# Up projections of the two convolution FFNs: 512-column matmuls from the third pair on, over an input that already holds the norm's factor

## Chip, cores and metric

The kernel runs on one core of one Trainium2 chip. The metric is the time of one execution on the device in microseconds (us). Engines are named as in the profile: PE is TensorE (matmuls), PEld its weight loads, DVE is VectorE, ACT is ScalarE, POOL is GpSimd, SP is SyncE, which issues the DMAs of the weights.

## What is computed

One sequence of 256 tokens with 1024 channels goes through seven phases: attention and pooling (L0), FFN F0, sliding-window attention (L1), FFN F1, then FFN F2, a mixer with convolution and attention (MIX), and FFN F3. All is in float32. The change touches F0 and F1, which the reference computes so:

```python
def rms_norm(x, g):
    xf = x.astype(jnp.float32)
    y = xf * lax.rsqrt(jnp.mean(xf * xf, axis=-1, keepdims=True) + EPS)
    return (y * g.astype(jnp.float32)).astype(x.dtype)

def conv_glu_ffn(x, norm_g, w_up, conv_w, conv_b, w_down):
    S = x.shape[1]
    h = rms_norm(x, norm_g) @ w_up
    hp = jnp.pad(h, ((0, 0), (CONV_W - 1, 0), (0, 0)))
    c = conv_b
    for j in range(CONV_W):
        c = c + conv_w[j] * hp[:, j:j + S]
    gate, up = jnp.split(c, 2, axis=-1)
    return x + (jax.nn.silu(gate) * up) @ w_down
```

`CONV_W` is 3, `w_up` is 1024 x 5632 and `w_down` 2816 x 1024. F2 and F3 have the same shapes, but no convolution.

## The kernel before

**Precision.** Every float32 product is made of three matmuls in the type fp32r: an operand is split into a high part (a copy in fp32r) and a low part (the operand less its high part), and high x high, high x low and low x high are summed in PSUM. Channels lie on the 128 partitions, tokens along the free axis, so an activation tile has 256 columns.

**Weights.** They come in 172 chunks, most of 128 x 2048 (1 MB). SP loads chunk i into one of 3 buffers `raw`, once the low part of chunk i-3 is made (`s_lo`). ACT makes the high part `whi` (`high(i)`, once PE is done with chunk i-4, `s_used`), DVE the low part `wlo` (`low(i)`). PE waits for `wlo` of a chunk before its first matmul with it.

**An FFN.** Chunks c0 to c0+21 are the up projection, two for each of 11 pairs p (two gate tiles in one, two up tiles in the other, by position e); chunks c0+22 to c0+32 are the down projection. In `half` (F0 and F1) a weight tile multiplies 256 columns at a time: three matmuls for each of 16 weight tiles of a chunk, result in one bank of 512 columns. In `wide` (F2 and F3) high and low activations lie side by side (`G2[:, k, :, :]`), so one matmul of 512 columns makes high x high and high x low in the two halves of a bank, and one of 256 columns makes low x high; the chunk's result takes two banks, and ACT copies the right halves out (`s_side`) before DVE adds the left ones (`s_ev`). The down projection is of the wide kind in F0, F1 and F2.

**The norm.** G is made from x times the gain, without the factor over the channels. PE sums the squares with a matmul of ones after pair 0 (`norm_sum`), ACT takes the square root (`Rt`, L1027), DVE the reciprocal (`R`, L1514), and in F0 and F1 DVE multiplies each result by R as it takes it out of PSUM into `Hb` (L1522, recorded at L1465).

**The convolution.** For each pair ACT makes the third tap with the bias (`Cb`, four instructions, L1035), DVE adds the other two (eight, recorded at L1471), ACT takes Silu (`gate`, L1010), POOL multiplies gate and up into `Ab` (L2107), ACT copies it to `Ahi` (`a_high`), and POOL makes `Alo` (L2107).

**Order.** Each engine goes through its program in order; the loops over p on ACT and DVE are the ones that the diff changes. On DVE a turn is: the lows of two later chunks (2 and 3 at p = 0; 4, 5 and 6 at p = 1; then 2p+3 and 2p+4), the two evictions into `Hb`, eight taps. SP also loads a table of 2 MB, `bias_c`, into the buffer `bias` in the middle of F0's weights. Lines L1465, L1471, L969, L2107 and L298 are helpers through which many operations of an engine go.

Of the kernel before, what the change touches and what calls it, by code (L numbers as in the profile page):

```python
# [12 lines left out]
DT = 8  # L13
# [79 lines left out]
L0, F0, L1, F1, F2, MIX, F3 = range(7)  # L93
FFNS = {F0: 0, F1: 1, F2: 2, F3: 3}
FIRST = {L0: 0, F0: 12, L1: 45, F1: 54, F2: 87, MIX: 120, F3: 135}
UNIT = {L0: 0, L1: 4, MIX: 12}
# [29 lines left out]
def program(nc, x, wst, par_d, cst_d, bias_a_d, bias_c_d, invcnt_d, wgroup_d, fin_d, out):  # L126
    ctx = ExitStack()
    with ctx:
# [101 lines left out]
        s_ev, s_t2, s_tap, s_silu = sem("s_ev"), sem("s_t2"), sem("s_tap"), sem("s_silu")  # L230
        s_side, s_cr = sem("s_side"), sem("s_cr")
        s_mul, s_ahi, s_alo, s_pad = sem("s_mul"), sem("s_ahi"), sem("s_alo"), sem("s_pad")

# [33 lines left out]
        def _(sp):  # L267
# [28 lines left out]
        def _(pe):  # L296
# [10 lines left out]

            def half(b, i, h, ph=None):

# [4 lines left out]
                for n in range(2):  # L314
                    for k in range(4 * h, 4 * h + 4):
                        if n == 0 and ph is not None:
                            pe.wait_ge(s_glo, 8 * ph + k + 1)
                        if n == 0 and i < 2 and k % 2 == 0:
                            pe.wait_ge(s_lo, k // 2 + 1 if i == 0 else 5 + k // 4)
                        ws = slice(n * P, n * P + P)  # L320
                        last = three(bank[b][:, n * S:n * S + S], h3[:, k, ws], l3[:, k, ws], Ghi[:, k, :], Glo[:, k, :],
                                     k == 0 and n == 0, k == DT - 1)
                if h == 1:
                    last.then_inc(s_used, 1)

            def wide(b, i, h, ph=None):

# [4 lines left out]
                for n in range(2):  # L332
                    for k in range(4 * h, 4 * h + 4):
                        if n == 0 and ph is not None:
                            pe.wait_ge(s_glo, 8 * ph + k + 1)
                        ws = slice(n * P, n * P + P)
                        mm(bank[b + n], h3[:, k, ws], G2[:, k, :, :].rearrange("p a s -> p (a s)"), k == 0, False)
                        last = mm(bank[b + n][:, 0:S], l3[:, k, ws], G2[:, k, 0, :], False, k == DT - 1)
# [85 lines left out]

            def up_conv(ph, frees):
                n = FFNS[ph]
                c0 = FIRST[ph]
                for p in range(FP):
                    banks = [at(ph, 4 + 2 * (p % 2) + e) for e in range(2)]
                    for e in range(2):  # L430
                        if p < 2:
                            frees(4 + 2 * p + e)
                        else:
                            pe.wait_ge(s_ev, 22 * n + 2 * (p - 2) + e + 1)
                        if p > 0:
                            half(banks[e], c0 + 2 * p + e, 0)
                            half(banks[e], c0 + 2 * p + e, 1)
                        else:
                            half(banks[e], c0 + e, 0, ph if e == 0 else None)
                    if p == 0:  # L440
                        for e in range(2):
                            half(banks[e], c0 + e, 1, ph if e == 0 else None)
                        norm_sum(ph, False)

# [20 lines left out]
            def ffn(ph, frees):  # L465
# [12 lines left out]
                def out_free(b):  # L478

                    if ph in (F0, F1):  # L480
                        if b == 3:
                            pe.wait_ge(s_rt, ph + 1)
                        elif b >= 4:
                            pe.wait_ge(s_ev, 22 * n + (21, 22, 19, 20)[b - 4])
                    elif b % 2 == 0:
                        pe.wait_ge(s_ev, 22 * n + 19 + b // 2)
# [475 lines left out]
        def _(act):  # L962
# [17 lines left out]
            def residual(ph):  # L980
                nxt = ph + 1
                for j in (0, 2):
                    for j_ in (j, j + 1):
                        act.wait_ge(s_x, 4 * ph + j_ + 1)
                        for n in (2 * j_, 2 * j_ + 1):
                            act.activation(Ghi[:, n, :], X[:, n, :], ACT.Identity, scale=col(GAIN[nxt], n)).then_inc(s_ghi, 1)
                    for j_ in (j, j + 1):
# [11 lines left out]
            def ffn(ph):  # L999
# [4 lines left out]
                def gate(p):  # L1004
# [5 lines left out]
                    act.activation(Cb[:, b, 0:2, :], Cb[:, b, 0:2, :], ACT.Silu).then_inc(s_silu, 1)  # L1010

                def a_high(p):
                    act.wait_ge(s_mul, FP * n + p + 1)
                    copy(Ahi[:, 2 * p:2 * p + 2, :], Ab[:, p % 2, :, :]).then_inc(s_ahi, 1)

                for p in range(FP):
# [6 lines left out]
                    if p >= 1:  # L1023
                        gate(p - 1)
                    if p == 0:
                        act.wait_ge(s_nrm, ph + 1)
                        act.activation(Rt[:, :], bank[at(ph, 3)][:, 0:S], ACT.Sqrt, bias=eps[:, 0:1], scale=1.0 / 1024).then_inc(s_rt, 1)  # L1027
                    if conv is not None:
                        for e in range(4):
                            ch = (e // 2) * FT + 2 * p + e % 2  # L1030
# [6 lines left out]
                    else:  # L1037
                        for e in range(2):
                            b = at(ph, 4 - 4 * (p % 2)) + 2 * e
                            act.wait_ge(s_used, USED[c0 + 2 * p + e])  # L1040
                            if e == 0 and p >= 2:
                                act.wait_ge(s_mul, FP * n + p - 1)
                            copy(Cb[:, p % 2, 2 * e:2 * e + 2, :], psum[:, b:b + 2, S:512]).then_inc(s_side, 1)
                a_high(FP - 2)
# [416 lines left out]
        def _(dve):  # L1461
# [16 lines left out]
            def residual(ph):  # L1478
# [14 lines left out]
                def lows(j):  # L1493
                    for n in (2 * j, 2 * j + 1):
                        dve.wait_ge(s_ghi, 8 * nxt + n + 1)
                        STT(Glo[:, n, :], X[:, n, :], col(GAIN[nxt], n), f(Ghi[:, n, :]), ALU.mult, ALU.subtract).then_inc(s_glo, 1)

# [6 lines left out]
            def ffn(ph):  # L1504
                n = FFNS[ph]
                conv = n if n < 2 else None
                c0 = FIRST[ph]
                for p in range(FP):
# [3 lines left out]
                    if p == 0:  # L1512
                        dve.wait_ge(s_rt, ph + 1)
                        dve.reciprocal(R[:, :], Rt[:, :]).then_inc(s_R, 1)  # L1514
                    for e in range(2):
                        if conv is not None:
                            dve.wait_ge(s_used, USED[c0 + 2 * p + e])
                            if p == 0 and e == 0:
                                dve.wait_ge(s_R, n + 1)
                            if p >= 2 and e == 0:  # L1520
                                dve.wait_ge(s_tap, 8 * (FP * n + p - 1))
                            TT(Hb[:, b, 2 * e:2 * e + 2, 2:S + 2], two(bank[at(ph, 4 + 2 * b + e)][:, :]), Rb(), ALU.mult).then_inc(s_ev, 1)  # L1522
                        else:
                            o, b0 = Cb[:, b, 2 * e:2 * e + 2, :], at(ph, 4 - 4 * b) + 2 * e
                            dve.wait_ge(s_side, 2 * (FP * (n - 2) + p) + e + 1)
                            TT(o, psum[:, b0:b0 + 2, 0:S], o, ALU.add).then_inc(s_ev, 1)
# [5 lines left out]
                    if conv is not None:  # L1532
                        if p == 0:
                            dve.wait_ge(s_pad, n + 1)
                        for tap in (1, 0):
                            for e in range(4):
                                ch = (e // 2) * FT + 2 * p + e % 2
                                if tap:
                                    dve.wait_ge(s_t2, 4 * (FP * n + p) + e + 1)
                                else:  # L1540
                                    dve.wait_ge(s_tap, 8 * (FP * n + p) + e + 1)
                                STT(Cb[:, b, e, :], Hb[:, b, e, tap:tap + S], col(f"conv{conv}", tap * 44 + ch),
                                    Cb[:, b, e, :], ALU.mult, ALU.add).then_inc(s_tap, 1)
                for j in range(FP - 1):
# [796 lines left out]
```

## Time and profile before

| | |
|---|---|
| median of 3 runs | 1066.82 us (1065.29 to 1067.52) |
| the profiled execution, its own time | 1067.42 us |
| its span in the profile | 1065.6 us |
| PE busy | 1027.7 us, 96% |
| DVE busy | 732.4 us, 69% |
| ACT busy | 609.0 us, 57% |
| POOL busy | 345.7 us, 32% |
| share of PE in the chain that ended last | 85% |

A row of the timeline gives the start of a group of instructions on an engine, the time that it took, the engine, the line, the operation with its output and inputs, and the count; a bracket at the end tells how long the engine was idle before it and who released it, and a row without one began as soon as the engine was free. The recorded durations of matmuls overlap, so their pace is read from the distance between starts.

### The profile page before, as it was taken

Reading aid. Unit: us, or ns where it says so; the run is one execution under the profiler, and the core shown is the slowest. Engines: PE = TensorE matmul, PEld = TensorE weight load, DVE = VectorE, ACT = ScalarE, POOL = GpSimd, SP = SyncE. Lnnn points to the kernel's source line nnn. Section 1 sums busy time; section 2 is a strip of 40 time slices with the busy share of each in tenths; the row PEclk is TensorE's granted clock in tenths of the full one; section 3 lists DMA queues with packets and bytes.
Section 4 is the critical chain, followed back from the end, with each engine's and each line's share of the span. In section 5 each row is a group of like instructions: output and inputs, shape, how many; then the busy total and the mean of one; then the engine's idle time right before and its main releaser. Section 6 shows DMA issues by size and latency. Waiting matters only on the chain.

```text
span 1065.6 us, 17048 instructions
## 1 busy us (share of the span) xinstructions
PE 1027.7 (96%) x7078; PEld 941.7 (88%) x7078; DVE 732.4 (69%) x992; ACT 609.0 (57%) x841; POOL 345.7 (32%) x189
## 2 busy tenths in 40 slices
PE   6999999999999899999999999999999799999997
PEld 5889999998888799999888888888899598888886
DVE  5876898775548779887647766653799778666543
ACT  6765656653356657565436655543667776555631
POOL 1061264540000024545202455510148413555300
PEclk9999999999999999999999999999999899999999
DMA  8544665446432255555554655555245136555451
GB/s 320 205 147 141 255 212 185 166 151 237 159 119 80 69 189 198 205 191 164 197 193 141 242 186 181 198 197 193 102 160 167 72 120 219 190 183 197 139 177 40
DMA packets 27292, 183.53 MB, mean 172 GB/s; under 512 B 3152, under 2 KB 3280, under 8 KB 5968
## 3 DMA queue, kind: packets, MB, share of 16 engines
q1 hardware_dynamic: 26784, 181.74, 48.5%
q8 instruction: 56, 0.92, 0.3%
q10 hardware_dynamic: 432, 0.71, 0.2%
q14 instruction: 20, 0.16, 0.0%
HBM read 181.39 MB, written 1.05 MB: 171 GB/s over the span
## 4 chain that ended last, share of the span: by engine, by line
PE 85%; ACT 4%; DVE 4%; issue 3%; POOL 2%; DMA 1%; SPq 0%; DVEq 0%; POOLq 0%; ACTq 0%
PE psum L298 84%; POOL Y L2107 2%; ACT Pb L1075 1%; DVE Pb L1572 1%; DMA raw<-in_wst 1%; DVE wlo L1465 1%; ACT whi L969 1%; ACT Ob L1273 1%; DVE X L1471 1%; ACT Pb L1282 0%; DVE bias L1471 0%; DVE Pb L1468 0%; ACT PT L969 0%; PE psum L530 0%; POOL acc L2107 0%
## 5 line engine op out<-in xcount | busy, mean ns | idle before, releaser
L298 PE MATMUL psum<-G,whi 128*128 128x256 f32 (+1 forms) x2720 | 613.0, 313 | 9.7 <-DVE wlo L1465 9.7
L1465 DVE TENSOR_TENSOR wlo<-raw,whi 128x2048 fp32r<-128x2048 f32 (+1 forms) x172 | 389.3, 2275 | 205.0 <-ACT whi L969 204.9
L298 PEld LDWEIGHTS psum<-G,whi 128*128 128x128 f32 x2720 | 445.6, 190 | 44.2 <-DVE G L1471 8.4
L298 PE MATMUL psum<-G,wlo 128*128 128x256 f32 x1712 | 481.1, 281 | 0.0
L969 ACT ACTIVATE whi<-raw 128x2048 fp32r<-128x2048 f32 (+1 forms) x172 | 318.8, 1866 | 173.5 <-PE psum L298 164.4
L298 PEld LDWEIGHTS psum<-G,wlo 128*128 128x128 f32 x1712 | 324.1, 189 | 0.1
L298 PE MATMUL psum<-A,whi 128*128 128x512 f32 x528 | 183.2, 392 | 0.0
L2107 POOL TENSOR_TENSOR A<-Ab,A 128x512 fp32r<-128x512 f32 x44 | 124.9, 2839 | 139.6 <-ACT A L969 139.6
L2107 POOL TENSOR_TENSOR Ab<-Cb 128x512 f32<-128x512 f32 x44 | 117.5, 2670 | 116.1 <-ACT Cb L1010 116.1
L298 PE MATMUL psum<-A,wlo 128*128 128x256 f32 x528 | 147.3, 279 | 0.0
L298 PEld LDWEIGHTS psum<-A,whi 128*128 128x128 f32 x528 | 98.8, 187 | 22.0
L2107 POOL TENSOR_TENSOR acc<-sq 128x512 f32<-128x512 f32 x7 | 9.1, 1298 | 319.5 <-ACT sq L990 303.3
L298 PEld LDWEIGHTS psum<-A,wlo 128*128 128x128 f32 x528 | 99.6, 189 | 0.0
L1035 ACT ACTIVATE Cb<-Hb,par 128x256 f32<-128x256 f32 x88 | 47.4, 595 | 61.6 <-DVE Hb L1465 61.6
L1471 DVE SCALAR_TENSOR_TENSOR Cb<-Hb,par,Cb 128x256 f32<-128x256 f32 x176 | 78.0, 503 | 0.9
L298 PE MATMUL psum<-Mhi,whi 128*128 128x256 f32 x192 | 55.5, 289 | 1.0 <-DVE Mlo L1465 1.0
L298 PE MATMUL psum<-whi,A 128*128 128x512 f32 x176 | 54.6, 390 | 0.0
L298 PE MATMUL psum<-Mhi,wlo 128*128 128x256 f32 x192 | 54.3, 283 | 0.0
L298 PE MATMUL psum<-Mlo,whi 128*128 128x256 f32 x192 | 54.3, 283 | 0.0
L969 ACT ACTIVATE Cb<-psum 128x512 f32<-128x512 f32 x44 | 25.7, 589 | 48.5 <-PE psum L298 48.5
L2107 POOL TENSOR_TENSOR Y<-Y,Ob 128x256 f32<-128x256 f32 x41 | 41.6, 1015 | 12.2 <-ACT Ob L1273 4.7
L1465 DVE TENSOR_TENSOR Cb<-psum,Cb 128x512 f32<-128x512 f32 x44 | 29.8, 684 | 22.9 <-ACT Cb L969 22.9
(176 smaller groups left out, 1005.5 us busy)
## 6 DMA issues: line engine op xcount, KB each, us to landing
raw<-in_wst SPq DMA_DIRECT2D x165, 1024.0 KB, 4.9
bias<-in_bias_c SPq DMA_DIRECT2D x1, 2048.0 KB, 8.7
raw<-in_wst SPq DMA_DIRECT2D x3, 512.0 KB, 7.5
X<-in_x SPq DMA_DIRECT2D x4, 256.0 KB, 6.6
raw<-in_wst SPq DMA_DIRECT2D x4, 256.0 KB, 6.9
out<-bias SPq DMA_DIRECT2D x4, 256.0 KB, 2.0
bias<-in_bias_a SPq DMA_DIRECT2D x1, 512.0 KB, 11.1
bias<-in_invcnt SPq DMA_DIRECT2D x1, 512.0 KB, 12.0
```

The source lines that it names most:

```text
L298: return pe.matmul(o, a, b, start=start, stop=stop, skip_group_check=True)
L969: return act.activation(o, i, ACT.Copy)
L1035: act.activation(Cb[:, p % 2, e, :], Hb[:, p % 2, e, 2:S + 2], ACT.Identity, scale=col(f"conv{conv}", 2 * 44 + ch), bias=col(f"convb{conv} ...
L1075: last = act.activation(Pb[:, e, m, c0:c1], Pb[:, e, m, c0:c1], ACT.Exp, bias=st[:, e, 4 + k_:5 + k_], accum_out=st[:, e, 8 + k_:9 + k_])
L1273: act.activation(PR[:, q % 4, :], UP[:, i, j:j + S], ACT.Copy, scale=col("conv_w", 4 * j + i)).then_inc(s_prod, 1)
L1465: return dve.tensor_tensor(o, a, b, op)
L1471: return dve.scalar_tensor_tensor(o, a, s, b, op0, op1)
L1572: dve.tensor_tensor_reduce(Pb[:, e, m, c0:c1], bank[banks[m]][:, c0:c1], bias_of(m)[:, S - nk:S], 1.0, init_of(m), ALU.add, ALU.max, st[:, ...
L2107: return pool.tensor_tensor(o, a, b, op)
```

## The change

In F0 and F1 the first two pairs stay with 256-column matmuls, now into banks 0 to 3, and read x times the gain from `E2`, a part of the buffer `A2` that is not yet in use. From the third pair on (`NARROW = 2`) the chunks go through `wide`. Their input is not x times gain but x times gain times R: DVE makes it in `Yn` (the upper half of `bias`), ACT and DVE split it into `G2`. R comes from Ln and Exp on ACT in place of the square root and the reciprocal. ACT copies the right halves of the wide results into `Hb` (`side`), and DVE adds the left ones. The load of `bias_c` moves by four chunks and waits for the low parts of the normed input.

```diff
+NARROW = 2
+            E2 = A2[:, FT - DT:FT, :, :]
+        Yn = upper
...
             for i in range(3, NCH):
-                if i == FIRST[F0] + 5:
-                    sp.wait_ge(s_glo, 8 * F0 + 8)
+                if i == FIRST[F0] + 9:
+                    sp.wait_ge(s_nlo, 2)
                     sp.dma_start(bias[:, :], bias_c_d).then_inc(s_bc, 16)
...
             def up_conv(ph, frees):
-                for p in range(FP):
-                    banks = [at(ph, 4 + 2 * (p % 2) + e) for e in range(2)]
+                for e in range(2):
+                    half(at(ph, e), c0 + e, 0, ph if e == 0 else None, E2)
+                for e in range(2):
+                    half(at(ph, e), c0 + e, 1, ph if e == 0 else None, E2)
+                norm_sum(ph, False)
+                for e in range(2):
+                    if e == 1:
+                        pe.wait_ge(s_rt, ph + 1)
+                    half(at(ph, 2 + e), c0 + 2 + e, 0, None, E2)
+                    half(at(ph, 2 + e), c0 + 2 + e, 1, None, E2)
+                for p in range(NARROW, FP):
                     for e in range(2):
+                        if p == NARROW:
+                            frees(4 + 2 * e)
+                            frees(5 + 2 * e)
+                        elif p == NARROW + 1:
+                            pe.wait_ge(s_ev, 22 * n + 2 * e + 2)
                         else:
                             pe.wait_ge(s_ev, 22 * n + 2 * (p - 2) + e + 1)
+                        b = at(ph, 4 - 4 * (p % 2)) + 2 * e
+                        for h in range(2):
+                            wide(b, c0 + 2 * p + e, h, None, n if p == NARROW and e == 0 else None)
...
+                def side(p, e):
+                    act.wait_ge(s_used, USED[c0 + 2 * p + e])
+                    if conv is not None:
+                        b, o = at(ph, 4 - 4 * (p % 2)) + 2 * e, Hb[:, p % 2, 2 * e:2 * e + 2, 2:S + 2]
+                        if e == 0:
+                            act.wait_ge(s_tap, 8 * (FP * n + p - 1))
...
+                    copy(o, psum[:, b:b + 2, S:512]).then_inc(s_side, 1)
+
+                def normal_high(h):
+                    act.wait_ge(s_yn, 2 * n + h + 1)
+                    ks = slice(4 * h, 4 * h + 4)
+                    copy(Ghi[:, ks, :], Yn[:, ks, :]).then_inc(s_nhi, 1)
...
+                def normal(h):
+                    for k in range(4 * h, 4 * h + 4):
+                        last = STT(Yn[:, k, :], X[:, k, :], col(GAIN[ph], k), R[:, :], ALU.mult, ALU.mult)
+                    last.then_inc(s_yn, 1)
+
+                def normal_low(h):
+                    dve.wait_ge(s_nhi, 2 * n + h + 1)
+                    ks = slice(4 * h, 4 * h + 4)
+                    TT(Glo[:, ks, :], Yn[:, ks, :], f(Ghi[:, ks, :]), ALU.subtract).then_inc(s_nlo, 1)
...
                         low(c0 + i)
+                        if conv is not None and i == 4:
+                            taps(0, 0)
+                    if p == 0 and conv is not None:
+                        dve.wait_ge(s_R, n + 1)
+                        normal(0)
+                        normal(1)
...
+                        if conv is not None and p >= NARROW:
+                            o, b0 = Hb[:, b, 2 * e:2 * e + 2, 2:S + 2], at(ph, 4 - 4 * b) + 2 * e
+                            dve.wait_ge(s_side, SIDE[n, p, e])
+                            TT(o, psum[:, b0:b0 + 2, 0:S], o, ALU.add).then_inc(s_ev, 1)
```

DVE's program at the start of F0, before the change: the lows of chunks 2 and 3, the reciprocal, pair 0's evictions and taps, the lows of chunks 4 to 6, pair 1's evictions.

```order
L1465 TENSOR_TENSOR wlo<-raw,whi 128x2048 [waits s_hi] x2
L1514 RECIPROCAL R<-Rt 128x256 [waits s_rt]
L1465 TENSOR_TENSOR Hb<-psum,R 128x2x256 [waits s_R,s_used]
L1465 TENSOR_TENSOR Hb<-psum,R 128x2x256 [waits s_used]
L1471 SCALAR_TENSOR_TENSOR Cb<-Hb,par,Cb 128x256 [waits s_t2,s_pad]
L1471 SCALAR_TENSOR_TENSOR Cb<-Hb,par,Cb 128x256 [waits s_t2] x3
L1471 SCALAR_TENSOR_TENSOR Cb<-Hb,par,Cb 128x256 [waits s_tap] x4
L1465 TENSOR_TENSOR wlo<-raw,whi 128x2048 [waits s_hi] x3
L1465 TENSOR_TENSOR Hb<-psum,R 128x2x256 [waits s_used] x2
```

The same place on DVE after the change; `bias` here is `Yn`, the row with `G<-bias,G` the low part of the normed input.

```order
L1504 TENSOR_TENSOR wlo<-raw,whi 128x2048 [waits s_hi] x2
L1510 SCALAR_TENSOR_TENSOR bias<-X,par,R 128x256 [waits s_R]
L1510 SCALAR_TENSOR_TENSOR bias<-X,par,R 128x256 x7
L1504 TENSOR_TENSOR Hb<-psum,R 128x2x256 [waits s_used] x2
L1504 TENSOR_TENSOR G<-bias,G 128x4x256 [waits s_nhi] x2
L1510 SCALAR_TENSOR_TENSOR Cb<-Hb,par,Cb 128x256 [waits s_t2,s_pad]
L1510 SCALAR_TENSOR_TENSOR Cb<-Hb,par,Cb 128x256 [waits s_t2] x3
L1504 TENSOR_TENSOR wlo<-raw,whi 128x2048 [waits s_hi]
L1510 SCALAR_TENSOR_TENSOR Cb<-Hb,par,Cb 128x256 [waits s_tap] x4
L1504 TENSOR_TENSOR wlo<-raw,whi 128x2048 [waits s_hi] x2
L1504 TENSOR_TENSOR Hb<-psum,R 128x2x256 [waits s_used] x2
```

Eight instructions for `Yn` and two for `G` now stand ahead of chunk 4's low part, the reciprocal is gone, and four of pair 0's taps moved behind that low part.

ACT's program from the square root to pair 0's third taps and the high parts of chunks 4 to 6, before the change.

```order
L1027 ACT_TABLE_LOAD
L1027 ACTIVATE Rt<-psum,eps 128x256 [waits s_nrm]
L1035 ACTIVATE Cb<-Hb,par 128x256 [waits s_ev]
L1035 ACTIVATE Cb<-Hb,par 128x256
L1035 ACTIVATE Cb<-Hb,par 128x256 [waits s_ev]
L1035 ACTIVATE Cb<-Hb,par 128x256
L969 ACTIVATE whi<-raw 128x2048 [waits s_used,s_raw1]
```

And after it.

```order
L978 ACT_TABLE_LOAD
L1059 ACTIVATE Rt<-psum,eps 128x256 [waits s_nrm]
L1061 ACTIVATE R<-Rt 128x256 [waits s_rt]
L981 ACTIVATE G<-bias 128x4x256 [waits s_yn] x2
L1078 ACTIVATE Cb<-Hb,par 128x256 [waits s_ev]
L1078 ACTIVATE Cb<-Hb,par 128x256
L1078 ACTIVATE Cb<-Hb,par 128x256 [waits s_ev]
L1078 ACTIVATE Cb<-Hb,par 128x256
L981 ACTIVATE whi<-raw 128x2048 [waits s_used,s_raw1]
```

One instruction makes R, two make the high part of the normed input, all ahead of pair 0's third taps and of chunk 4's high part.

## Rows read from the trace of the kernel before

**Rows 1.** The page: busy time, share, count of PE.

```profile
PE 1027.7 (96%) x7078; PEld 941.7 (88%) x7078; DVE 732.4 (69%) x992; ACT 609.0 (57%) x841; POOL 345.7 (32%) x189
```

**Rows 2.** The chain that ended last, in order of time: start, us, what.

```profile
75.14 236.15 PE psum L298 x1794
...
376.65 373.49 PE psum L298 x2492
```

**Rows 3.** Timeline of PE in F0: first matmuls of pair 0 and of pair 1.

```profile
100.64 0.40 PE L298 MATMUL psum<-G,whi 128*128 128x256 f32 x2
...
112.41 0.59 PE L298 MATMUL psum<-G,whi 128*128 128x256 f32 x2
```

**Rows 4.** Timeline of PE in F2, a wide chunk.

```profile
610.26 0.40 PE L298 MATMUL psum<-G,whi 128*128 128x512 f32 x1
610.49 0.28 PE L298 MATMUL psum<-G,wlo 128*128 128x256 f32 x1
```

**Rows 5.** Timeline of ACT in F0, the same step four pairs apart.

```profile
171.12 1.10 ACT L1035 ACTIVATE Cb<-Hb,par 128x256 f32<-128x256 f32 x2 [0.45 <-DVE Hb L1465]
...
217.20 1.10 ACT L1035 ACTIVATE Cb<-Hb,par 128x256 f32<-128x256 f32 x2 [0.45 <-DVE Hb L1465]
```

**Rows 6.** Timeline of ACT in F2, the same step seven pairs apart.

```profile
615.66 0.60 ACT L969 ACTIVATE Cb<-psum 128x512 f32<-128x512 f32 x1 [2.57 <-PE psum L298]
...
693.31 0.60 ACT L969 ACTIVATE Cb<-psum 128x512 f32<-128x512 f32 x1 [2.57 <-PE psum L298]
```

**Rows 7.** Timeline of DVE at the start of F0.

```profile
113.30 1.75 DVE L1514 RECIPROCAL R<-Rt 128x256 f32<-128x256 f32 x1 [2.32 <-ACT Rt L1027]
115.16 1.29 DVE L1465 TENSOR_TENSOR Hb<-psum,R 128x512 f32<-128x512 f32 x2
116.59 3.48 DVE L1471 SCALAR_TENSOR_TENSOR Cb<-Hb,par,Cb 128x256 f32<-128x256 f32 x8
119.99 6.69 DVE L1465 TENSOR_TENSOR wlo<-raw,whi 128x2048 fp32r<-128x2048 f32 x3
126.59 1.29 DVE L1465 TENSOR_TENSOR Hb<-psum,R 128x512 f32<-128x512 f32 x2
```

**Rows 8.** Timeline of ACT at the start of F0.

```profile
112.80 0.47 ACT L1027 ACTIVATE Rt<-psum,eps 128x256 f32<-128x256 f32 x1 [4.26 <-PE psum L298]
115.89 2.08 ACT L1035 ACTIVATE Cb<-Hb,par 128x256 f32<-128x256 f32 x4 [2.62 <-DVE Hb L1465]
117.87 5.51 ACT L969 ACTIVATE whi<-raw 128x2048 fp32r<-128x2048 f32 x3
```

**Rows 9.** Timeline of ACT in L1: the Exp of a factor R.

```profile
299.31 0.42 ACT L997 ACTIVATE R<-Rt 128x256 f32<-128x256 f32 x1
```

**Rows 10.** Groups by line and shape: count, busy us, mean ns, idle before.

```profile
L969 ACT ACTIVATE Cb<-psum 128x512 f32<-128x512 f32 x44 | 25.7, 589 | 48.5 <-PE psum L298 48.5
...
L969 ACT ACTIVATE whi<-raw 128x1024 fp32r<-128x1024 f32 x3 | 3.2, 1056 | 1.0 <-DMA raw<-in_wst 1.0
...
L1465 DVE TENSOR_TENSOR Cb<-psum,Cb 128x512 f32<-128x512 f32 x44 | 29.8, 684 | 22.9 <-ACT Cb L969 22.9
```

**Rows 11.** Timeline of DVE and POOL in F0: a pair without idle time.

```profile
135.82 1.29 DVE L1465 TENSOR_TENSOR Hb<-psum,R 128x512 f32<-128x512 f32 x2
...
146.82 1.28 DVE L1465 TENSOR_TENSOR Hb<-psum,R 128x512 f32<-128x512 f32 x2
...
144.72 3.35 POOL L2107 TENSOR_TENSOR Ab<-Cb 128x512 f32<-128x512 f32 x1
```

**Rows 12.** DMA: the table's landing time (issues), and one stretch (windows).

```profile
bias<-in_bias_c SPq DMA_DIRECT2D x1, 2048.0 KB, 8.7
...
106.00:109.00 3.00, 3.00 (x27) 3.00 (x26) 3.00 (x2) 2.52 (x2) 2.80 (x3) 1.00 1.00 421
```

**Rows 13.** Timeline at the start of F1: the square root, chunk 4's low part.

```profile
394.63 0.48 ACT L1027 ACTIVATE Rt<-psum,eps 128x256 f32<-128x256 f32 x1 [3.29 <-PE psum L298]
...
401.83 6.68 DVE L1465 TENSOR_TENSOR wlo<-raw,whi 128x2048 fp32r<-128x2048 f32 x3
```

More of the change, by code:

```diff
@@ L94 @@
 FFNS = {F0: 0, F1: 1, F2: 2, F3: 3}
+NARROW = 2
+SIDE = place(*[(n, p, e) for n in range(4) for p in range(NARROW if n < 2 else 0, FT // 2) for e in range(2)])
 FIRST = {L0: 0, F0: 12, L1: 45, F1: 54, F2: 87, MIX: 120, F3: 135}
@@ L231, in program @@
         s_side, s_cr = sem("s_side"), sem("s_cr")
+        s_yn, s_nhi, s_nlo = sem("s_yn"), sem("s_nhi"), sem("s_nlo")
         s_mul, s_ahi, s_alo, s_pad = sem("s_mul"), sem("s_ahi"), sem("s_alo"), sem("s_pad")
@@ L306, in weights, with half @@
                 return (v[:, i % NH, 0:widths[i]].rearrange("p (k n) -> p k n", k=k) for v in (whi, wlo))
-            def half(b, i, h, ph=None):
+            def half(b, i, h, ph=None, G=G2):
                 h3, l3 = weights(i, DT)
@@ L320, in half @@
                         ws = slice(n * P, n * P + P)
-                        last = three(bank[b][:, n * S:n * S + S], h3[:, k, ws], l3[:, k, ws], Ghi[:, k, :], Glo[:, k, :],
+                        last = three(bank[b][:, n * S:n * S + S], h3[:, k, ws], l3[:, k, ws], G[:, k, 0, :], G[:, k, 1, :],
                                      k == 0 and n == 0, k == DT - 1)
@@ L324, in half, with wide @@
                     last.then_inc(s_used, 1)
-            def wide(b, i, h, ph=None):
+            def wide(b, i, h, ph=None, normed=None):
                 h3, l3 = weights(i, DT)
@@ L335, in wide @@
                             pe.wait_ge(s_glo, 8 * ph + k + 1)
+                        if n == 0 and normed is not None:
+                            pe.wait_ge(s_nlo, 2 * normed + k // 4 + 1)
                         ws = slice(n * P, n * P + P)
@@ L985, in residual @@
                         for n in (2 * j_, 2 * j_ + 1):
-                            act.activation(Ghi[:, n, :], X[:, n, :], ACT.Identity, scale=col(GAIN[nxt], n)).then_inc(s_ghi, 1)
+                            act.activation((E2 if nxt in (F0, F1) else G2)[:, n, 0, :], X[:, n, :], ACT.Identity,
+                                           scale=col(GAIN[nxt], n)).then_inc(s_ghi, 1)
                     for j_ in (j, j + 1):
@@ L1024, in ffn @@
                         gate(p - 1)
-                    if p == 0:
+                    if p == 0 and conv is not None:
+                        table()
+                        act.wait_ge(s_nrm, ph + 1)
+                        act.activation(Rt[:, :], bank[at(ph, 3)][:, 0:S], ACT.Ln, bias=eps[:, 0:1], scale=1.0 / 1024).then_inc(s_rt, 1)
+                        act.wait_ge(s_rt, ph + 1)
+                        act.activation(R[:, :], Rt[:, :], ACT.Exp, scale=-0.5).then_inc(s_R, 1)
+                    elif p == 0:
                         act.wait_ge(s_nrm, ph + 1)
@@ L1037, in ffn @@
                     else:
[L1038 to L1043, printed above, removed]
+                        side(p, 0)
+                        side(p, 1)
                 a_high(FP - 2)
@@ L1495, in lows @@
                         dve.wait_ge(s_ghi, 8 * nxt + n + 1)
[L1496 removed]
+                        g = E2 if nxt in (F0, F1) else G2
+                        STT(g[:, n, 1, :], X[:, n, :], col(GAIN[nxt], n), f(g[:, n, 0, :]), ALU.mult, ALU.subtract).then_inc(s_glo, 1)
                 for j in (0, 2):
@@ L1507, in ffn, with taps @@
                 c0 = FIRST[ph]
+                def normal(h):
[6 more added lines that the diff above has]
+                    TT(Glo[:, ks, :], Yn[:, ks, :], f(Ghi[:, ks, :]), ALU.subtract).then_inc(s_nlo, 1)
+                def taps(p, tap):
+                    if p == 0 and tap:
+                        dve.wait_ge(s_pad, n + 1)
+                    for e in range(4):
+                        ch = (e // 2) * FT + 2 * p + e % 2
+                        if tap:
+                            dve.wait_ge(s_t2, 4 * (FP * n + p) + e + 1)
+                        else:
+                            dve.wait_ge(s_tap, 8 * (FP * n + p) + e + 1)
+                        STT(Cb[:, p % 2, e, :], Hb[:, p % 2, e, tap:tap + S], col(f"conv{conv}", tap * 44 + ch),
+                            Cb[:, p % 2, e, :], ALU.mult, ALU.add).then_inc(s_tap, 1)
                 for p in range(FP):
@@ L1511, in ffn @@
                         low(c0 + i)
-                    if p == 0:
+                        if conv is not None and i == 4:
+                            taps(0, 0)
+                    if p == 0 and conv is not None:
+                        dve.wait_ge(s_R, n + 1)
+                        normal(0)
+                        normal(1)
+                    elif p == 0:
                         dve.wait_ge(s_rt, ph + 1)
@@ L1533, in ffn @@
                         if p == 0:
[L1534 to L1543, printed above, removed]
+                            normal_low(0)
+                            normal_low(1)
+                        taps(p, 1)
+                        if p > 0:
+                            taps(p, 0)
                 for j in range(FP - 1):
```

38 lines of the change are left out of this document (14 added, 24 removed).

## The prediction

> **What bounds the kernel now.** I read the page first: PE is busy for 96% of the span [rows 1]. Busy alone proves little, so the chain of waits in order of time came next. It holds two long pieces that are PE alone, 236.15 us from 75.14 and 373.49 us from 376.65 [rows 2]. F0 begins at 100.64 [rows 3] and lies in the first, F1 and F2 in the second. So in the stages that the change touches nothing is waited for: the time is the number of matmuls times their pace. Then I took the pace from starts, since durations of matmuls overlap. In F0 the same step of ACT comes at 171.12 and four pairs later at 217.20 [rows 5]: 11.52 us a pair, 5.76 a chunk, 0.360 for the three matmuls of a weight tile, 0.120 for one of 256 columns. In F2, where the up projection is wide already, the same step comes at 615.66 and seven pairs later at 693.31 [rows 6]: 11.093 a pair, 5.546 a chunk, 0.3467 a weight tile, of which the 512-column matmul takes about 0.23 [rows 4]. The columns streamed are equal (768), so the difference, 13.3 ns, is what one matmul less saves. The granted clock is 1.00 in F0 [rows 12], the 2.4 GHz level: there 256 columns would last 106.7 ns, and the other 13.3 ns of the 120 are paid for each matmul. The two readings agree.
>
> **What the change saves.** Pairs 2 to 10 of two FFNs are 18 pairs, 36 chunks, 576 weight tiles. 18 x (11.52 - 11.093) = 7.69 us; as a check 576 x 13.3 ns = 7.7. It all lies on the path [rows 2]. The down projections and the first two pairs keep their matmuls.
> Here the Trainium skill speaks against the change: "TensorE: Matmul & The Clock Gate", section "Back-to-back issue gap", gives an isolated warm matmul N / 2.4 GHz plus 2.5 ns, by which 576 fewer would save an estimated 1.4 us. It says itself that weight loads add to that spacing, and this trace has 13.3 ns where the page has 2.5.
>
> **What it adds in a steady pair.** ACT gets two copies out of PSUM of 0.589 each [rows 10]; DVE's two evictions stay two: an addition of 0.684 [rows 10] for a multiplication at 1.29 for two [rows 7]. DVE's pair is then 1.3 for evictions, 3.5 for eight taps, 2 x 2.2 for lows (three starts in 119.99 to 126.59, [rows 7]), 9.2 in all if nothing disturbs it, against PE's 11.09. With POOL working beside it, DVE took 11.0 without a pause, from 135.82 to 146.82, while a POOL multiplication lasted 3.35 [rows 11]. Both are below 11.09, so I charge nothing; the cover is thin, 0.1 us a pair at worst. The eviction is a two-step now: after PE ends a pair the copy takes 0.6, the addition 0.7, 1.3 in all. Behind it stand on DVE the taps and the lows of chunks three and four ahead, on ACT the third taps and the highs. PE wants those banks a whole pair later, 11 us, and the next low chunks 5.5 or more later. At the start of the down projection PE needs bank 6 after 12 weight tiles, 4.2 us after the end of the up projection, and has it after 1.3. Nothing there either.
>
> **What it adds at the start of F0.** This is the term I expect to cost, and it is a chain of single steps. Ln stands where the square root does: 112.80 + 0.47 = 113.27 [rows 8]. Exp takes 0.42 [rows 9]: R is there at 113.72, while before it was there at 115.05, after a reciprocal of 1.75 [rows 7]. DVE's eight instructions for `Yn`, with the shape of the taps, take 3.48 [rows 7]: 117.2. Two evictions of pair 0: 1.29, until 118.45. ACT copied the second half of `Yn` meanwhile: 117.2 + 1.06 for a copy of 128 x 1024 [rows 10] = 118.3. Two subtractions of 128 x 1024, half a low each, 1.1: until 120.65. The first four taps, half of 3.48: 122.4. On ACT: 118.3, four third taps 2.08, the high part of chunk 4 1.84 [rows 8]: 122.2, just in time. Low part of chunk 4: 122.4 + 2.2 = 124.6, before the change 122.2 [rows 7]. PE begins pair 1 at 112.41 [rows 3] and ends it 11.52 later, at 123.93. There it wants the normed input (120.65, 3.3 us early) and the low part of chunk 4 (124.6, 0.7 late). So PE waits some 0.6 us. Bounds: 0 if the steps without POOL beside them run 0.1 quicker each, and 2 if `Yn` or the halves of 1024 cost a quarter more and PE restarts slowly. Late next: four taps 1.7 and the low of chunk 5 until 128.5, wanted at 124.6 + 5.5 = 130.1; chunk 6 until 130.7, wanted at 135.7; pair 1's taps, then chunk 7 until about 138.4, wanted at 141.2. The margins are 1.6, 5 and 2.8, and they do not shrink afterwards as long as DVE stays below 11.09 a pair. Pair 4 reuses pair 2's banks at 146.8; they are empty at about 141.
> In F1 the steps are the same: from the square root to chunk 4's low part it is 119.99 - 112.80 = 7.19 in F0 and 401.83 - 394.63 = 7.20 in F1 [rows 7, 8, 13]. Again 0.6.
>
> **The moved load.** `bias_c` landed 8.7 us after its issue, and one stretch carried 421 GB/s [rows 12], 5.0 us for 2 MB. It now stands before chunk 9's weights. SP issues chunk 8's load after chunk 5's low, at 128.5, the table at once (its wait ended at 120.7), chunk 9's after chunk 6's low, at 130.7. Four MB at 421 GB/s, 10 us, and 2 or 3 us of latency: chunk 9 lands at 141. ACT comes to it after pair 2's third taps, at about 143, and PE wants it at 152.4. The move costs nothing. The two places in which SP waits (for `s_nlo`, for `s_lo`) hold nothing else up.
>
> **The sum.** -7.7 + 2 x 0.6 = -6.5. On the profiled execution's own 1067.42 that is 1060.9; its time is 0.6 above the median of the three, so on the median it is 1060.3 (-0.61%).
>
> **Rivals.**
> *No stall at all* (12%): each start step is a little quicker, PE finds chunk 4 ready. 1066.8 - 7.7 = 1059.1. For it: the miss is only 0.7 us. Against it: no step has slack, the chain goes through DVE without a gap.
> *A start that costs more* (12%): DVE's late lows meet POOL's first multiplication and the table's 2 MB, chunk 5 (margin 1.6) and chunk 7 (2.8) are late too, 1.5 to 3 us an FFN in place of 0.6. For it: rows 11 show lows and taps together stretched from 9.2 to 11.0 beside POOL. Against it: POOL has nothing before pair 0's Silu. 1059.1 + 2 x 1.5 to 2 x 3: 1062 to 1065.
> *DVE and ACT become the bound, slower than before* (4%): the copy on ACT ahead of each addition puts two waits of 0.6 into DVE's turn when DVE is already behind, so that its full 11.0 [rows 11] becomes 12.2. PE then runs at 12.2 instead of 11.09: over 9 pairs 10.0 us, less the lead of 2.8, 7.2 an FFN, 14.4 in two; 1066.8 - 7.7 + 14.4 = 1073.5. It decides at a pair of 11.8: (11.8 - 11.09) x 9 - 2.8 = 3.6 an FFN eats the gain. For it: in that pair DVE had no pause. Against it: a DVE that is behind finds the copies already made.
> By the Trainium skill, "GPSIMD Engine Reference", section "Specifications", GpSimd's SBUF interface contends with DVE instructions that have two SBUF inputs; the slow pair of rows 11 agrees.
> *The matmul saved is worth nearly nothing* (2%): the wide chunk's pace in F2 comes from something else in F2. Then only the stalls of 1.2 remain: 1068. Against it: the 0.3467 also holds in rows 4, matmul by matmul.
>
> **How the numbers follow.** The forecast as worked out, with 0.2 to 1.2 us of stall an FFN, has 70%: 1059.5 to 1061.5. With no stall it is 1059.1, and a single set of runs moves by about 1 (those shown spread over 2.2). From 1058.7 to 1062.8 these hold a good 8 in 10; the rest is the costly start and the slow case. Faster by over 0.2% (2.1 us, about what a measurement of this kernel can tell): 70 + 12 + 12 = 94%. Slower: 4%. Same: 2%.
>
> **What the changed profile would show.** 576 matmuls fewer. The same step of ACT or DVE 11.09 us apart in F0 and F1 from pair 2 on, as in F2. One wait of PE for DVE's `wlo` (chunk 4) of about 0.6 us at the start of pair 2 in F0 and one in F1, none for `G`, none for `Hb`. DVE's share up, with idle time left between the lows. Chunk 9's high part not waiting for its DMA. The prediction is wrong if pairs in F0 lie 11.3 or more apart, or if PE waits at every pair; then DVE's turn is the place to look.

## The result and the profile after

The changed kernel took 1062.91 us at the median of 5 runs (1061.27 to 1063.68), the kernel before 1065.74 in the same set (1065.29 to 1067.52): ratio 0.9965, 95% interval 0.9954 to 0.9976. That is 2.8 us or 0.35% less, where 6.5 us or 0.61% were forecast. The profiled execution took 1063.31 with a span of 1061.5.

The page after, its first lines, against [rows 1]:

```profile
span 1061.5 us, 15952 instructions
...
PE 1023.6 (96%) x6502; PEld 910.5 (86%) x6502; DVE 745.1 (70%) x1010; ACT 629.5 (59%) x883; POOL 357.7 (34%) x189
```

PE has 6502 matmul records for 7078: the 576 fewer that the prediction counted. Its busy time fell by 4.1 us, not by 7.7.

The chain that ended last, in order of time, where [rows 2] had two pieces:

```profile
74.94 37.63 PE psum L304 x304
...
124.32 183.41 PE psum L304 x1106
...
373.06 29.46 PE psum L304 x242
402.77 343.72 PE psum L304 x1962
```

F0's matmuls began at 100.64 before and the piece that holds them, with L1's first ones, ended at 311.29; after, they begin at 100.44 and it ends at 307.73: 210.7 before, 207.3 after, 3.4 less. So F0 gave what was forecast for it (3.84 less a wait). From F1's beginning to F2's end it was 750.14 - 382.47 = 367.7 before, and is 746.49 - 378.89 = 367.6 after. F1 gave nothing. No wait explains it: from F1's first matmul to F2's end PE waits once in the up projection, for 0.24 us, at the third pair:

```profile
402.77 0.47 PE L304 MATMUL psum<-G,whi 128*128 128x512 f32 x1 [0.24 <-DVE wlo L1504]
```

The pace does. ACT's copy of a pair's last chunk, the same step as in [rows 6], in F0 and in F1:

```profile
157.88 0.60 ACT L981 ACTIVATE Hb<-psum 128x512 f32<-128x512 f32 x1 [0.86 <-PE psum L304]
...
168.97 0.60 ACT L981 ACTIVATE Hb<-psum 128x512 f32<-128x512 f32 x1 [2.07 <-PE psum L304]
...
448.27 0.60 ACT L981 ACTIVATE Hb<-psum 128x512 f32<-128x512 f32 x1 [2.68 <-PE psum L304]
...
459.57 0.60 ACT L981 ACTIVATE Hb<-psum 128x512 f32<-128x512 f32 x1 [2.67 <-PE psum L304]
```

A pair takes 11.09 us in F0, as in F2 before [rows 6], and 11.30 in F1. The difference is there from matmul to matmul. PE's timeline at F0's third pair, later in F0, and in F1:

```profile
124.32 0.47 PE L304 MATMUL psum<-G,whi 128*128 128x512 f32 x1 [0.25 <-DVE wlo L1504]
...
160.46 0.39 PE L304 MATMUL psum<-G,whi 128*128 128x512 f32 x1
160.69 0.28 PE L304 MATMUL psum<-G,wlo 128*128 128x256 f32 x1
160.80 0.39 PE L304 MATMUL psum<-G,whi 128*128 128x512 f32 x1
...
460.43 0.40 PE L304 MATMUL psum<-G,whi 128*128 128x512 f32 x1
460.67 0.28 PE L304 MATMUL psum<-G,wlo 128*128 128x256 f32 x1
460.79 0.40 PE L304 MATMUL psum<-G,whi 128*128 128x512 f32 x1
```

From tile to tile it is 0.346 at 160.46 and 0.36 at 460.43 (the rows round to 0.01). Over all tiles of a stretch the mean distance is 0.3467 in F0, and 0.3533 from 402.77, the first wide tile of F1, to 578, where F2's norm sum stands; then 0.3467 again. In the slow stretch every third distance is 0.361 and the two between are 0.349 and 0.350, so that three tiles take 20 ns more than three tiles of F0. The clock is not the reason. The windows of PE in the two stretches give time, busy time, count, granted clock, share of the DMA engines and GB/s, and the clock is 1.00 in both:

```profile
124.00:285.00 161.00, 160.75 (x928) 1.00 0.60 216
403.00:578.00 175.00, 175.00 (x992) 1.00 0.53 187
```

F1 has 464 wide tiles, F2 32 before its norm sum: 496 x 6.6 ns = 3.3 us. That is what is missing.

The start of F0 on DVE, against [rows 7]:

```profile
113.55 3.26 DVE L1510 SCALAR_TENSOR_TENSOR bias<-X,par,R 128x256 f32<-128x256 f32 x8 [2.78 <-ACT R L1061]
116.73 1.28 DVE L1504 TENSOR_TENSOR Hb<-psum,R 128x512 f32<-128x512 f32 x2
117.92 2.35 DVE L1504 TENSOR_TENSOR G<-bias,G 128x1024 fp32r<-128x1024 f32 x2
120.19 1.67 DVE L1510 SCALAR_TENSOR_TENSOR Cb<-Hb,par,Cb 128x256 f32<-128x256 f32 x4
121.78 2.29 DVE L1504 TENSOR_TENSOR wlo<-raw,whi 128x2048 fp32r<-128x2048 f32 x1
```

Chunk 4's low part ends at 124.07, forecast was 124.6, and PE is kept by it until 124.32.

### The profile page after: what moved, and what is told of

Same layout as the page of the kernel before. It is cut to its first block, busy times and chain, and to the rows that moved or that the text cites. A ratio compares the mean times of both kernels' runs of the same rounds, so it can differ in the third digit from the quotient of the medians.

```text
span 1061.5 us, 15952 instructions
## 1 busy us (share of the span) xinstructions
PE 1023.6 (96%) x6502; PEld 910.5 (86%) x6502; DVE 745.1 (70%) x1010; ACT 629.5 (59%) x883; POOL 357.7 (34%) x189
## 4 chain that ended last, share of the span: by engine, by line
PE 84%; DVE 5%; ACT 5%; issue 3%; POOL 2%; DMA 1%; SPq 0%; DVEq 0%; POOLq 0%; ACTq 0%
PE psum L304 83%; POOL Y L2170 2%; DVE wlo L1504 1%; ACT Pb L1114 1%; DVE Pb L1635 1%; DMA raw<-in_wst 1%; ACT whi L981 1%; ACT Ob L1312 1%; DVE bias L1510 1%; DVE X L1510 1%; ACT Pb L1321 0%; DVE Pb L1507 0%; ACT PT L981 0%; PE psum L542 0%; POOL acc L2170 0%
## 5 line engine op out<-in xcount | busy, mean ns | idle before, releaser
L304 PE MATMUL psum<-G,whi 128*128 128x512 f32 (+1 forms) x1888 | 560.9, 361 | 9.9 <-DVE wlo L1504 9.9
L304 PE MATMUL psum<-G,wlo 128*128 128x256 f32 x1584 | 443.2, 280 | 0.0
L304 PEld LDWEIGHTS psum<-G,whi 128*128 128x128 f32 x1888 | 335.9, 189 | 70.1 <-DVE G L1510 8.4
L304 PEld LDWEIGHTS psum<-G,wlo 128*128 128x128 f32 x1584 | 299.8, 189 | 0.1
L304 PE MATMUL psum<-A,whi 128*128 128x512 f32 (+1 forms) x784 | 231.0, 359 | 0.0
L2170 POOL TENSOR_TENSOR A<-Ab,A 128x512 fp32r<-128x512 f32 x44 | 141.6, 3218 | 132.7 <-ACT A L981 132.7
L304 PE MATMUL psum<-A,wlo 128*128 128x256 f32 x656 | 183.7, 280 | 0.0
L304 PEld LDWEIGHTS psum<-A,whi 128*128 128x128 f32 x784 | 138.8, 188 | 23.3
L304 PEld LDWEIGHTS psum<-A,wlo 128*128 128x128 f32 x656 | 123.9, 189 | 0.0
L1510 DVE SCALAR_TENSOR_TENSOR Cb<-Hb,par,Cb 128x256 f32<-128x256 f32 x176 | 82.9, 528 | 0.7
```

Source lines behind the costliest of these rows:

```text
L304: return pe.matmul(o, a, b, start=start, stop=stop, skip_group_check=True)
L1510: return dve.scalar_tensor_tensor(o, a, s, b, op0, op1)
L2170: return pool.tensor_tensor(o, a, b, op)
```

## Experiments

The question is why F1 is slow. Theory A: PE has two paces for the stream of wide tiles, set where the stream starts. Rival B: something of the changed F1 (its banks, its buffers, the work beside it) slows it. In each profile I took the distances between the 512-column matmuls' starts from end to end.

**1. The changed kernel again** (no edit).

> The changed kernel once more, unaltered, with a profile of its own. In the profiled execution of it every weight tile of a wide chunk (a 512-column matmul and one of 256) takes 0.3467 us in F0, but 0.3534 from the wait at the start of F1's third pair to the norm sum of F2, some 496 tiles, 3.3 us in all. Theory A (PE has two paces for this stream, and which one holds is set where it starts again after a wait or an odd matmul): the stretches at 0.3534 may lie elsewhere or be gone in another execution, and the time moves by up to 3.3 us with them; if the start is the same to the nanosecond they come again. Rival B (something of F1 itself is slow: its banks, its buffers, the work of ACT and DVE beside it): the same 0.3534 in F1 in every profile.

Measured: 1065.45 (11 runs, 1063.42 to 1066.11), ratio 0.9987 (0.9978 to 0.9996). The profiled execution took 1065.74, and F0 is now slow as well: every wide tile of F0, of F1 and of F2 up to its norm sum is at 0.3533. The chain's piece that ends F0 is longer:

```profile
124.17 186.45 PE psum L304 x1106
```

183.41 in the first profile, 186.45 here, for the same 1106 matmuls: 3.0 us more for 464 tiles. The start at 124.17 has the same wait (0.24). So the pace is no property of the program, and B would have to hold for F0 in one execution and not in another. Two slow FFNs gave next to nothing: F0's stretch is 210.33 us (0.3 less than in the kernel before), F1's and F2's 367.60 (0.1 less). Most of the 1.4 us by which the median lies below the kernel before is therefore not theirs (see experiment 7).

**2. No wait at the third pair.**

Chunk 4's high and low part move ahead of pair 0's taps, and the loops leave them out at their old places (shortened):

```diff
 ACT:  normal_high(1)
+      high(c0 + 4)
       ... third taps of pair 0
 DVE:  normal_low(1)
+      low(c0 + 4)
       taps(0, 1); taps(0, 0)
```

> Chunk 4's high part moves ahead of pair 0's third taps on ACT, its low part ahead of pair 0's first taps on DVE, in F0 and F1. The low part is then ready at about 1.6 us before PE asks for it, and PE enters the third pair without a wait. Theory A: no start after a wait, so F1 keeps 0.3467 as its down projection did in the kernel before; saved are 2 x 0.25 us of waits with some 0.2 us each of restart, and 3.3 us of pace: about 1059.3, 0.994 of the kernel before. Rival B: F1 stays at 0.3534, only 0.5 to 1 us are saved against the changed kernel: 1062. My prediction's sum for no stall at all was 1059.1.

Measured: 1065.37 (11 runs), ratio 0.9986 (0.9977 to 0.9995). PE goes into the wide stream without a wait, and both FFNs run at 0.3533 in the profile. Theory A in its first form, a restart after a wait, fell: a wait is not needed. Experiments 1 and 2 are both slow in F0 and F1, so they compare cleanly for the wait: from F0's first matmul to the end of the chain's piece it is 74.87 + 235.33 - 100.37 = 209.83 here and 124.17 + 186.45 - 100.29 = 210.33 there. The wait with its restart cost 0.50 us.

**3. One more fp32r matmul ahead of F1's down projection.**

```diff
+                    if ph == F1 and j == 0 and b == 0:
+                        mm(o[:, 0:S], l3[:, 0, ws], A2[:, 0, 0, :], True, False)
```

> The changed kernel with one extra matmul of 256 columns in front of F1's down projection (its result is overwritten by the next one, which starts the bank anew). Theory A: the odd matmul may move PE from 0.3534 back to 0.3467 for the 176 tiles of the down projection and 32 of F2: 1.4 us less, of which the extra matmul takes 0.12. Rival B: no change of pace, 0.12 us more.

Measured: 1066.18 (10 runs), ratio 0.9991 (0.9982 to 1.0001), unclear by itself. In the profile F0 and F1 are slow, the odd matmul shows as one distance of 0.47, and the third of 0.36 goes on behind it.

**4. The kernel before with four waits of PE.**

```diff
+                        if p == 3 and e == 0:
+                            pe.wait_ge(s_ev, 22 * n + 2 * (p - 1) + 2)
...
+                        if b == 0:
+                            pe.wait_ge(s_ev, 22 * n + 22)
```

> The kernel before the change, with four waits of PE put in: at the first matmul of the down projections of F0 and F1 (for the eviction of the last pair) and at pair 3 of F2 and F3 (for the eviction of pair 2). Each costs about 1.3 to 2 us by itself, 6 to 8 in all. Everywhere in the kernel before these stretches run at 0.3467 a tile (but for a short one at F3's start). Theory A: after some of the four waits the pace is 0.3534 until the next odd matmul; a stretch of 200 to 450 tiles then costs 1.4 to 3 us more. Rival B: all four keep 0.3467, since nothing else of F1's change is in this kernel.

Measured: 1076.43 (4 runs), ratio 1.0087 (1.0072 to 1.0103). Behind the waits at the down projections of F0 and F1 and in F2 the pace was 0.3533, behind the one in F3 0.3467. The one in F2 fell into a stretch that had run at 0.3467 since the norm sum. PE's timeline there:

```profile
610.68 0.50 PE L298 MATMUL psum<-G,whi 128*128 128x512 f32 x1 [1.41 <-DVE Cb L1469]
611.02 0.28 PE L298 MATMUL psum<-G,wlo 128*128 128x256 f32 x1
611.14 0.40 PE L298 MATMUL psum<-G,whi 128*128 128x512 f32 x1
...
611.50 0.40 PE L298 MATMUL psum<-G,whi 128*128 128x512 f32 x1
```

0.36 between the last two, and 0.3533 as a mean for the rest of F2. Nothing of F1's change is in this kernel: B is out. Behind a wait the fast pace can turn into the slow one. The sum fits too: waits of 0.9, 0.9, 1.4 and 1.4 us and some 815 tiles with 6.6 ns more each are 10.0 us, and the median rose by 9.6.

**5. One float32 matmul behind the first wide chunk.** In every profile the slow pace had ended at a norm sum, which is a float32 matmul and no fp32r one.

```diff
+                        if p == NARROW and e == 1:
+                            mm(bank[b][:, 0:S], ones, acc[:, 0:S], True, True)
```

> The changed kernel with one more float32 matmul of 128 x 256 (ones and the sum of squares, the same operands as the norm sum's, into a bank that the next chunk starts anew) between the first and the second wide chunk of F0 and of F1. So far the slow pace of 0.3534 us a tile was met from the first wide tile on, with a wait ahead of it or without one, it survived an extra fp32r matmul, and it ended in every profile at a norm sum, a float32 matmul. Theory A2 (the pace is drawn anew when the stream is entered or interrupted, and after a float32 matmul it comes out fast): the 16 tiles of the first chunk may run at 0.3534, all later ones of F0 and F1 at 0.3467; some 900 tiles, up to 6 us less than in a profile in which both are slow, for 2 x 0.25 us: about 1060. Rival B (F0 and F1 have something of their own that slows their wide tiles): 0.3534 behind the float32 matmul too, and 0.5 us more than the changed kernel: 1066.

Measured: 1060.45 (5 runs, 1060.04 to 1061.58), ratio 0.9946 (0.9933 to 0.996). Every wide tile of F0, F1 and F2 in the profile is at 0.3467, those of the first chunk too. So this profile shows no switch, since the pace was fast ahead of the float32 matmul already; the five times, all below every one of the 32 runs of experiments 1 to 3, speak for it.

**6. The same, and no wait.**

The edits of 2 and 5 together.

> The float32 matmul of the run before together with chunk 4's high and low parts moved ahead, so that PE does not wait at the third pair. Theory A2: as the run before, less some 0.4 us for each of the two waits: 1059.3. Rival B: 1065.5.

Measured: 1060.42 (5 runs, 1060.18 to 1060.7), ratio 0.9943 (0.9931 to 0.9956). This profile has the switch in it, in both FFNs. PE's timeline in F0:

```profile
128.31 0.40 PE L304 MATMUL psum<-G,whi 128*128 128x512 f32 x1
...
128.68 0.40 PE L304 MATMUL psum<-G,whi 128*128 128x512 f32 x1
...
129.74 0.59 PE L304 MATMUL psum<-acc,cst 128*128 128x256 f32 x2
129.98 0.58 PE L304 MATMUL psum<-G,whi 128*128 128x512 f32 x1
...
130.87 0.39 PE L304 MATMUL psum<-G,whi 128*128 128x512 f32 x1
...
131.21 0.40 PE L304 MATMUL psum<-G,whi 128*128 128x512 f32 x1
...
131.56 0.39 PE L304 MATMUL psum<-G,whi 128*128 128x512 f32 x1
```

The first chunk has distances of 0.36 at every third tile (128.31 to 128.68, rounded); behind the float32 matmul, two recorded passes at 129.74, they are 0.34 and 0.35, 0.3467 in the mean. In F1 it is the same. The float32 matmul takes 0.25 us itself (129.74 to 129.98), and the tile behind it 0.19 more than a fast one (129.98 to 130.51): 0.44 an FFN.

**7. The kernel before again** (no edit).

> The kernel before the change, unaltered, with a profile of its own. Its 27 other times lie in two groups, around 1065.4 and 1067.1. In its first profile (1067.42) the wide tiles of both down projections ran at 0.3467. Theory A2: a down projection may run at 0.3534 in this one (176 tiles, 1.2 us; in F1 with 32 tiles of F2, 1.4); the two groups then differ by one such draw, or by something in MIX, whose length differed by 2 us among the profiles. Rival B: both down projections at 0.3467 again, and always.

Measured: 1067.23 (11 runs, 1065.32 to 1067.94), ratio 1.0 (0.9992 to 1.0009). Both down projections at 0.3467 again, in an execution of the quicker group (1065.32). So between these two profiles of the kernel before the pace is not what differs. They differ in MIX, from the end of F2 to F3's long piece 750.14 to 848.20 in the first profile, 98.1 us, and 750.01 to 846.11, 96.1 us, here:

```profile
376.52 373.49 PE psum L298 x2492
...
846.11 154.89 PE psum L298 x938
```

TensorE's granted clock differs there. The same stretch of MIX in PE's windows, the first profile's row ahead, this one's behind it:

```profile
840.00:844.00 4.00, 3.68 (x16) 0.50 0.54 227
840.00:844.00 4.00, 3.71 (x22) 1.00 0.52 213
```

In both profiles the clock falls to 0.50, the 1.2 GHz level, at 835 to 836, behind waits of PE of 1.5 and 2.3 us for ACT. It is back at 1.00, the 2.4 GHz level, at 839.3 here and only at 845.3 in the first. The twelve profiles bear it out: the seven with a dip of 10.2 us have 120.0 to 120.8 us from the start of F2's last matmul to F3's first, the five with a shorter one 118.4 to 119.2. Why the dip is long in one execution and short in another stays open. L1 has such a dip in some profiles too. In the changed kernel's first profile the clock was 1.00 at the end of L1, in experiment 1's it was 0.50 for some 3 us, and the piece of the chain there was 1.5 us longer (30.95 for 29.46):

```profile
376.10:379.40 3.30, 3.30 (x17) 0.50 0.04 15
...
375.93 30.95 PE psum L304 x242
```

The profiles of experiments 2, 5, 6 and 10 have this dip as well, the others not. In F0, F1 and F2 the clock is 1.00 in all twelve profiles, so the two paces are a thing apart from it. The dips move a kernel here by up to 2 us in MIX and 1.5 in L1, so medians of 5 are not sharper than about 1 us, and stages are compared better than whole times.

**8. The float32 matmul ahead of the first wide chunk, no wait.**

```diff
-                        if p == NARROW and e == 1:
+                        if p == NARROW and e == 0:
                             mm(bank[b][:, 0:S], ones, acc[:, 0:S], True, True)
```

> As the run with the float32 matmul and no wait, but the float32 matmul stands right ahead of the first wide chunk, not behind it. There the first 16 tiles of F0 and of F1 ran at the slow pace, with every third distance at 0.36 or 0.37 us, and all later ones at 0.3467. If what counts is that a float32 matmul stands ahead of the stream, the first 16 are fast too: 0.1 us less an FFN, 1060.2. If it has to stand within a stream that already runs, the slow pace is entered behind it and stays for all of F0 and F1: up to 6 us more, 1065.5.

Measured: 1059.24 (5 runs, 1057.95 to 1059.99), ratio 0.9927 (0.9915 to 0.994). The pace is 0.3467 from the first tile on, in F0 and F1. PE's timeline:

```profile
124.03 0.59 PE L304 MATMUL psum<-acc,cst 128*128 128x256 f32 x2
124.28 0.58 PE L304 MATMUL psum<-G,whi 128*128 128x512 f32 x1
124.69 0.28 PE L304 MATMUL psum<-G,wlo 128*128 128x256 f32 x1
...
125.16 0.39 PE L304 MATMUL psum<-G,whi 128*128 128x512 f32 x1
...
125.50 0.40 PE L304 MATMUL psum<-G,whi 128*128 128x512 f32 x1
```

This version has the lowest median of all kernels here. From F0's first matmul to the end of its piece of the chain, and from F1's to F2's end, it takes 3.4 us less each than the kernel before.

**9. Two fp32r matmuls in the float32 one's place** (behind the first wide chunk, no wait).

```diff
+                            for _ in range(2):
+                                mm(bank[b][:, 0:S], h3[:, 0, 0:P], G2[:, 0, 0, :], True, True)
```

> As the run with the float32 matmul behind the first wide chunk and no wait, but with two fp32r matmuls of 256 columns in its place (a float32 one is recorded as two passes of 256). If the type of the odd matmul counts, the stream stays at 0.3534 as behind the one extra fp32r matmul before: 1065.5. If any interruption at this place, or an even number of extra matmuls, redraws the pace, F0 and F1 go on at 0.3467 in some or all cases: 1060.3.

Measured: 1065.15 (11 runs), ratio 0.9985 (0.9976 to 0.9994); 0.3533 ahead of and behind the extra matmuls, to F2's norm sum. PE's timeline:

```profile
129.14 0.40 PE L304 MATMUL psum<-G,whi 128*128 128x512 f32 x1
...
129.50 0.63 PE L304 MATMUL psum<-G,whi 128*128 128x256 f32 x3
...
130.44 0.40 PE L304 MATMUL psum<-G,whi 128*128 128x512 f32 x1
130.68 0.28 PE L304 MATMUL psum<-G,wlo 128*128 128x256 f32 x1
130.80 0.40 PE L304 MATMUL psum<-G,whi 128*128 128x512 f32 x1
```

0.36 again from 130.44 to 130.80. Two fp32r matmuls of the same columns at the same place did not end the slow pace, in the profile or in any of the 11 runs (1063.95 to 1067.31), and the float32 matmul did.

**10. The changed kernel a third time** (no edit, one run).

> The changed kernel, unaltered, profiled a third time. Of its four stretches so far (F0 and F1 in two profiles) three were slow. If the pace is drawn in each execution, another mixture is possible; if only F0's was a lucky exception, both are slow here: 1065.5.

Measured: 1059.47, and F0 and F1 both at 0.3467. Its chain:

```profile
124.17 183.40 PE psum L304 x1106
...
404.08 340.43 PE psum L304 x1962
```

The last piece, from F1's third pair to the end of F2, is 340.43 for 343.72 in the first two profiles, with 1962 matmuls each: 3.29 us, the 496 tiles. The same program gave fast and slow (1063.31), slow and slow (1065.74), fast and fast (1059.47). The last two have the clock's dips alike, within 0.1 us in L1 and in MIX, and the 6.3 us between them are the 960 tiles. By stages this execution has what was forecast: F0's stretch takes 207.3 us for 210.7, F1's and F2's 364.3 for 367.7, 3.4 less each and 6.7 together. Experiment 8 has the same two stretches (207.3 and 364.3): its float32 matmul keeps the slow pace away, and gains nothing over a fast draw.

## Why the prediction came out as it did

The direction and most steps were right, the size was not: 1062.91 is 0.1 above the upper end of the stated range and 2.6 above the forecast, and against the kernel before in its own set 2.8 us were saved of 6.5. That it came even so near was luck: in the profiled execution one of two FFNs had the fast pace, and the same program had its median at 1065.45 in experiment 1. Step by step:

- *What bounds the kernel* held: PE, by number and pace of matmuls. No pair made PE wait in F0 or F1 beyond the third.
- *18 pairs x (11.52 - 11.093) = 7.69* is the term that was mis-sized. The number of matmuls saved was right (576), and 0.3467 a tile holds where the pace is fast. I took F2's pace for the pace of every wide stretch. It is one of two. At 0.3533 a pair is 11.30, the saving 0.22 a pair and not 0.43, and the down projections, which were always fast in the kernel before, become slow with it: 11 x 16 tiles x 6.6 ns = 1.2 us lost in each FFN, 0.2 in F2's first chunks. With one slow FFN 7.7 becomes 7.7 less 3.1 to 3.3, with two 7.7 less 6.4, 1.3, from which the waits still go. The profiles of experiments 1, 2 and 9 are the second kind, with medians 1.4 to 1.8 us below the kernel before; that of experiment 10 has neither FFN slow and saves 6.7 in the two stretches, the forecast's price. The float32 matmul of experiments 5 and 6 brings the fast pace, for some 0.4 us an FFN, and both lie 6.7 us below the kernel before in their set, for the 6.5 forecast.
- *The start of F0*: the chain of single steps was right, and its end was 0.5 early (124.07 for 124.6): 0.2 because F0 itself began earlier (100.44 for 100.64), 0.2 because `Yn` took 3.26 for 3.48. The wait with its restart cost 0.50 for 0.6 (experiments 1 and 2). *No PE wait at `G` or `Hb`* held.
- *What it adds in a steady pair*: DVE was late by some microseconds at first and worked without a pause, with evictions at 139.20, 149.09, 158.98 and 168.86: 9.9 a pair, between the undisturbed 9.2 and the 11.0 of [rows 11]. It had caught up by 169. Charging nothing was right; the slower rival (12.2 a pair) found no ground.
- *The moved load* landed 9.4 us after its issue, and ACT waited 0.23 for a chunk's DMA at 144.56, at no cost to PE.
- *The matmul saved is worth nearly nothing*, "the wide chunk's pace in F2 comes from something else in F2", had 2%. Its mechanism was nearer to the truth than its chance: the pace does depend on something other than the tile, and what I put against it, rows of F2 alone, could not show that.
- *The sign of being wrong*, pairs in F0 11.3 or more apart, came true in experiment 1 (32 tiles at 0.3533 are 11.31), but the place that it named to look, DVE's turn, was the wrong one: beyond the third pair PE waited for nothing.

What stays open: why the stream enters the slow pace in one execution and not in another; why the down projection of the kernel before, entered from 256-column matmuls without a wait, was fast in 4 of 4 stretches while F0's wide stream in experiment 2, entered likewise, was slow; and whether it is float32 itself, its two passes or the place where it stands that sets the pace. A norm sum stands ahead of pair 1 in F0 and F1 of the changed kernel too, and the slow pace began behind it all the same, after 32 tiles of 256-column matmuls.

## What to carry to other kernels

Take the pace of a stream from the distances of many starts in each stage where it runs, after the change too: a figure from one stage is not safe for the same instructions in another. When a stage gives nothing back though its instructions are gone and no wait is new, compare the pace before looking for a wait, and profile the same kernel more than once. Look at the granted clock of the stages that the change does not touch as well: a dip of it there moved the time here by as much as the change. On this kernel, a float32 matmul of 256 columns (0.44 us with what it delays, into a bank that is to be started anew) ahead of each of two long streams of alternating 512 and 256 column fp32r matmuls was worth 5 to 6 us against the slow pace.

## What the runs showed of the hardware

A stream of fp32r matmuls of 512 and 256 columns with a weight load for each, at a granted clock of 1.00, runs at 0.3467 or at 0.3533 us a tile. At 0.3533 three tiles take 20 ns more than at 0.3467, most of it on one of them (0.361, 0.349, 0.350). A pace, once taken, held for up to 496 tiles, through chunks, banks and from one FFN into the next. Fp32r matmuls put in did not end it (experiments 3 and 9), and waits of 0.9 to 1.4 us were followed by the slow pace in three of four cases (experiment 4). Directly behind a float32 matmul the fast one came each time: at F2's and F3's norm sums in all profiles (F3's first 32 tiles were slow in each of them, before the change too), and in F0 and F1 in experiments 5, 6 and 8.

TensorE's granted clock fell to 0.50 in MIX in both profiles of the kernel before, for 10.2 us in one and 3.4 in the other, and MIX was 2.0 us longer with the long dip.
